# Half of the gate and z projections of one hybrid decoder layer computed by Strassen's scheme in 2 x 2 block pairs

## The reference, cut to what matters

```
hn    = rms_norm(x, norm_mix)                       # 1024 tokens x 1024 channels
proj  = hn @ w_in + b_in                            # x_rnn, z_rnn, q/k/v, z_att, gates
gates = sigmoid(proj[..., OFF_GATES:])              # 2 branches x 1024 channels
...
att   = sum over 3 groups of softmax(lse) * out     # merge of three dilated window patterns
y_att = att * silu(z_att)                           # 512 channels
merged = gates[0] * (y_rnn @ w_o_rnn) + gates[1] * (y_att @ w_o_att)
x = x + merged @ w_out                              # then a second, gated embedding branch
```

## Time and profile before

| | |
|---|---|
| median of 3 runs | 1344.41 us (1344.07 to 1344.48) |
| the profiled execution's own time | 1344.83 us |
| its span | 1343.0 us |
| TensorE busy, of the span | 1331.1 us (99%) |
| VectorE, ScalarE, POOL busy | 785.6, 507.7, 532.5 us |
| gate sigmoids (L827) start | 757.6 to 983.2 us |

### The profile page before, as it was taken

The page is one execution under the profiler, slowest core; times in us unless marked ns, Lnnn a source line. Parts: engine busy times, 40 slices in busy tenths (PEclk is TensorE's granted clock), DMA queues, the critical chain, the costliest instruction groups (busy, mean ns, idle before and its releaser), DMA issues.

```text
span 1343.0 us, 17645 instructions
## 1 busy us (share of the span) xinstructions
PE 1331.1 (99%) x6262; PEld 1104.2 (82%) x6262; DVE 785.6 (58%) x1257; ACT 507.7 (38%) x1282; POOL 532.5 (40%) x500
## 2 busy tenths in 40 slices
PE   8999999999999999999999999999999999999998
PEld 6887888888888888888888888888888888888887
DVE  6799888842779666565665752158612566234323
ACT  7455646542434444344443688311200011223100
POOL 6975424404458334041340632343067317044020
PEclk9999999999999999999999999999999999999999
DMA  6232312322202032120310332376279635122111
GB/s 239 79 102 87 105 60 79 110 100 72 75 12 83 24 91 64 32 83 20 99 56 33 114 93 92 100 244 212 94 270 413 201 127 155 57 79 63 40 47 47
DMA packets 84471, 139.51 MB, mean 104 GB/s; under 512 B 10048, under 2 KB 41120, under 8 KB 84384
## 3 DMA queue, kind: packets, MB, share of 16 engines
q10 hardware_dynamic: 39936, 75.82, 15.9%
q1 hardware_dynamic: 44448, 62.56, 15.6%
HBM read 108.84 MB, written 29.51 MB: 103 GB/s over the span
## 4 chain that ended last, share of the span: by engine, by line
PE 90%; DVE 5%; issue 1%; ACT 1%; POOL 1%; DMA 0%; SPq 0%; POOLq 0%; DVEq 0%; ACTq 0%
PE bank L1268 28%; PE bank L1273 28%; PE bank L1272 28%; PE bank L1425 2%; PE bank L1405 2%; PE bank L1392 1%; PE bank L1414 1%; DVE xc L1002 1%; PE bank L1518 1%; POOL ring L542 0%; ACT L743 0%; DMA raw<-in_w_rnn_s 0%; DVE qkr L1110 0%; DVE qks L1111 0%; DVE ibuf L1029 0%
## 5 line engine op out<-in xcount | busy, mean ns | idle before, releaser
L542 POOL TENSOR_TENSOR ring<-raw,ring 128x512 fp32r<-128x512 f32 x221 | 311.7, 1410 | 725.9 <-PE bank L1273 642.5
L1268 PE MATMUL bank<-hn,ring 128*128 128x512 f32 x640 | 251.7, 393 | 1.5 <-DVE sgbuf L990 1.2
L1273 PE MATMUL bank<-hn,ring 128*128 128x512 f32 x640 | 249.4, 390 | 0.0
L1272 PE MATMUL bank<-hn,ring 128*128 128x512 f32 x640 | 249.2, 389 | 0.0
L1268 PE MATMUL bank<-ring,hn 128*128 128x512 f32 x576 | 232.6, 404 | 0.2 <-POOL ring L542 0.2
L1273 PE MATMUL bank<-ring,hn 128*128 128x512 f32 x576 | 225.8, 392 | 0.0
L1272 PE MATMUL bank<-ring,hn 128*128 128x512 f32 x576 | 225.2, 391 | 0.0
L546 POOL TENSOR_SCALAR ring<-raw 128x512 fp32r<-128x512 f32 x221 | 183.7, 831 | 8.4 <-DMA raw<-in_w_rnn_s 8.3
L1268 PEld LDWEIGHTS bank<-hn,ring 128*128 128x128 f32 x640 | 120.2, 188 | 26.7 <-DVE sgbuf L990 1.6
L1273 PEld LDWEIGHTS bank<-hn,ring 128*128 128x128 f32 x640 | 120.1, 188 | 25.3
L1272 PEld LDWEIGHTS bank<-hn,ring 128*128 128x128 f32 x640 | 120.2, 188 | 24.1
(11 more groups left out here) (182 smaller groups left out, 2151.9 us busy)
## 6 DMA issues: line engine op xcount, KB each, us to landing
raw<-in_w_tail_s SPq DMA_DIRECT2D x104, 256.0 KB, 2.7
g_in<-gate_dram ACTq DMA_DIRECT2D x48, 256.0 KB, 3.6
raw<-in_w_rnn_s SPq DMA_DIRECT2D x45, 256.0 KB, 2.6
raw<-in_w_qkv_s SPq DMA_DIRECT2D x48, 192.0 KB, 2.4
gate_dram<-g_out ACTq DMA_DIRECT2D x32, 256.0 KB, 2.1
raw<-in_w_qkv_s SPq DMA_DIRECT2D x48, 128.0 KB, 2.2
o_dram<-o_buf ACTq DMA_DIRECT2D x48, 128.0 KB, 1.8
o_in<-o_dram ACTq DMA_DIRECT2D x12, 512.0 KB, 3.9
```

What stands on the lines that cost most here:

```text
L542: nc.gpsimd.tensor_tensor(ring[:, ring_slot(p), 1], raw[:, p % RAW], ring[:, ring_slot(p), 0].bitcast(F32), ALU.subtract).then_inc(w_ready, 1)
L1268: ins = T.matmul(out, lhs[0], rhs[0], start=first, stop=False)
L1272: T.matmul(out, lhs[0], rhs[1], start=False, stop=False)
L1273: return T.matmul(out, lhs[1], rhs[0], start=False, stop=last)
```

## The change

The first eight gate tiles (`PLAIN`) stay as they are, in 16 slots. The other eight gate tiles and the four z tiles are taken two at a time, in six pairs (`PAIRS`): two output tiles by two token halves, with the 8 channel blocks split 4 and 4. Such a 2 x 2 by 2 x 2 product needs 8 block products; the change computes it with 7 (`PRODUCTS`), each of 4 blocks x 3 matmuls, from sums and differences of quadrants.

- Activation quadrants: VectorE makes three combinations per channel block (`combine`, 7 operations of 128 x 512 for each k, two after each of the attention steps that lie in gate slots), POOL cuts them into hi and lo in ring slots 4 to 15 (`combined_parts`, 6 operations each). A fourth combination overwrites a quadrant of `hn` (`combine_last`, 5 VectorE operations for each of 4 blocks).
- The ring has four slots for the gates and pairs (`RING_PAIR`).
- Weight quadrants: a pair's four pieces are loaded together (`load_pair`); POOL makes four sums in place in `raw`. From the fifth product on, ScalarE makes the hi part of each product's weights (`weight_hi`), POOL the lo part.
- Products go round eight banks. ScalarE copies the first product of a pair to `part_sum`; VectorE adds the others (7 additions per pair) into the four outputs, from which ScalarE takes the sigmoids.
- The merge steps are placed by a table (`MERGE_AT`) behind products 10 to 34, the merge weights at product 3. The weights are now stored by class, so that the multiplication in `merge_step` is one contiguous operation. The loads of `o_in`, `wt_in`, the statistics and merge weights move from ScalarE's queue to SP's, between the pairs' weight loads.

```diff
+PLAIN = 8
+GATE_ORDER = [(t, h) for t in range(PLAIN - 2) for h in range(2)] + [(t, h) for h in (1, 0) for t in (PLAIN - 2, PLAIN - 1)]
+PAIRS = [("z", 0), ("z", 2)] + [("gate", t) for t in range(PLAIN, 2 * KD, 2)]
+PRODUCTS = 7
+MERGE_AT = {10 + 9 * i // 4: i for i in range(UNITS)}
+ROWS_AT = 3
...
@@ sync @@
+            def load_pair(u):
+                for r in range(RAWS):
+                    sp.wait_ge(w_ready, FIRST_PAIR + PRODUCTS * (u - 1) + 3 + r + 1)
+                    load(raw_of(u, r), a["w_tail_s"][FIRST_PAIR - FIRST_TAIL + RAWS * u + r])
...
+            load_pair(1)
+            sp.wait_ge(mw_done, 1)
...
+            load_parts(0, 2)
+            load_pair(2)
+            load_parts(2, 4)
+            load_pair(3)
+            load_parts(4, 7)
+            load_pair(4)
+            load_parts(7, 10)
+            load_pair(5)
+            load_parts(10, UNITS)
@@ gpsimd @@
+                for r in range(2):
+                    pool.wait_ge(raw_in[slots[r]], pair_count(u, r))
+                    cut(r, r)
+                for r in (2, 3):
+                    pool.wait_ge(raw_in[slots[r]], pair_count(u, r))
+                G.tensor_tensor(a21, a21, a22, ALU.add).then_inc(pair_sum, 1)
...
+                G.tensor_tensor(a11, a21, a11, ALU.subtract).then_inc(pair_sum, 1)
...
+                G.tensor_tensor(a12, a12, a11, ALU.subtract).then_inc(pair_sum, 1)
...
+                cut(2, 0)
+                G.tensor_tensor(a11, a22, a11, ALU.subtract).then_inc(pair_sum, 1)
+                cut(3, 1)
+                cut(4, 0)
+                cut(5, 2)
+                cut(6, 3)
@@ scalar @@
+            for m in range(PRODUCTS * len(PAIRS) + 2):
+                u, i = divmod(m, PRODUCTS)
+                if u < len(PAIRS):
+                    act.wait_ge(prod_done, m + 1)
+                    if i == 0:
+                        if u >= 1:
+                            act.wait_ge(*pair_taken(u - 1, 0))
+                        nc.scalar.activation(part_sum[:, 0], pair_bank(u, 0)[:], ACT.Copy).then_inc(prod_kept, 1)
+                    if m + RING_PAIR < PRODUCTS * len(PAIRS):
+                        weight_hi(m + RING_PAIR)
...
+                    if i == 4:
+                        take_pair(u, 0)
+                if u >= 1 and i == 0:
+                    take_pair(u - 1, 1)
+                    take_pair(u - 1, 2)
+                if u >= 1 and i == 1:
+                    take_pair(u - 1, 3)
@@ vector @@
+                if i == 2:
+                    dve.wait_ge(prod_kept, u + 1)
+                    if u >= 1:
+                        dve.wait_ge(*pair_taken(u - 1, 2))
+                    link(V.tensor_tensor(u_sum, pair_bank(u, 2)[:], first, ALU.add))
+                    V.tensor_tensor(first, pair_bank(u, 1)[:], first, ALU.add).then_inc(prod_sum, 1)
...
+                if m in MERGE_AT:
+                    merge_step(MERGE_AT[m])
+                    if MERGE_AT[m] % GROUPS == GROUPS - 1:
+                        finish_head(MERGE_AT[m] // GROUPS)
@@ tensor @@
+            for m in range(PRODUCTS * len(PAIRS)):
+                u, i = divmod(m, PRODUCTS)
...
+                    pe.wait_ge(*product_taken(m - 8))
...
+                c = FIRST_PAIR + m
+                need(c)
+                moving = pair_moving(i)
+                for k in range(KD // 2):
+                    ins = passes(pair_bank(u, i)[:], part(c, slice(k * P, (k + 1) * P)), moving(k),
+                                 k == 0, k == KD // 2 - 1)
+                ins.then_inc(prod_done, 1)
+                used[0] = 1
```

More of the change, by code:

```diff
@@ L107, with combined_ops @@
 MAIN_ORDER = main_order()
-Q_STAT = 15
+Q_STAT = 14
+Q_FREE = GATE_ORDER.index((PLAIN - 1, 1))
+def combined_ops(A):
+    first = SLOTS_Q * KD
+    free = [a for a in range(STEPS) if FIRST_STEP + STEP_BLOCKS * a >= first]
+    if A not in free:
+        return range(0)
+    i = free.index(A)
+    return range(min(2 * i, 7 * KD // 2), min(2 * i + 2, 7 * KD // 2))
+COMBINE_AFTER = (5, 7, 9, 13)
+MERGE_AT = {10 + 9 * i // 4: i for i in range(UNITS)}
+ROWS_AT = 3
 P_CUT = (2, 4)
@@ L452, in evacuated @@
             if n < N_O:
-                q = n - N_Z
-                kind = Z_MAIN[q][0]
-                done = sum(1 for m in Z_MAIN[:q + 1] if m[0] == kind)
-                return (gate_done if kind == "gate" else za_done), done
+                return gate_done, n - N_Z + 1
             if n < N_W:
@@ L1116, in _ @@
                     attention(G)
+                    for j in combined_ops(G):
+                        combine(j)
                     continue
```

437 lines of the change are left out of this document (304 added, 133 removed).

## The result

| | kernel before | changed kernel |
|---|---|---|
| time, median of the comparison | 1344.41 us | 1368.3 us |
| lowest to highest run | 1344.07 to 1344.48 | 1368.23 to 1372.28 |
| profiled execution: time, span | 1344.83, 1343.0 | 1368.27, 1366.4 |

The ratio is 1.0183 with a 95% interval of 1.0171 to 1.0196: 24 us slower, where 1330.0 us and 14 us faster were forecast. The case that came true is the second rival, and it was worse than its 1356 us.

A forecast was written before the change was run, and what follows sets the result against it. TensorE's number of matmuls times their pace was taken as the bound. 1344.83 - 16.3 saved + 2 for waits gave 1330.5 us profiled; the median, 0.42 us lower, was forecast at 1330.0 us, range 1327.5 to 1340.

The forecast's parts named there:

- the second rival: Also rival 2: in the merge stretch VectorE and POOL shut each other out, 28 us surplus, 1356 us; chance 0.09.
- The saving: Six pairs on TensorE drop 72 matmuls at 0.2267 us, saving 16.3 us; a pair takes 19.04 us.
- the weighing of the rule: VectorE's two-SBUF-input instructions block POOL's SBUF reads, or the reverse; judged contradicted at 904.44, where both seemed to run at once.
- Its sign, a mean of POOL above 2 us: POOL's mean operation time in the pairs: above 2 us would show mutual exclusion; 1.4 to 1.6 was expected for lo parts.
- POOL's margin of 1.75 us: POOL's 11 operations per pair: TensorE waits only above about 1.75 us an operation; the mean was taken as 1.565.
- VectorE's drift "under the 8 us": Merge stretch: VectorE has 73 us of work in 68, drifts some 5 us behind, and may be 8 us late.
- ScalarE's waits for its sums: In the pairs ScalarE waits for VectorE's sums with the next hi part queued behind; cost 0.
- The combinations at cost 0: Beside the last attention steps, VectorE's two operations, 1.5 us, fit its 2.81 us idle per step; cost 0.
- SP's queue: Third pair's weights, issued at 29 to 31 us behind merge loads, cost 1 us of the 2 us charged.
- "Later pairs have their merge loads early enough": Pairs after the third: their merge loads come early enough in SP's queue, so no late weights were charged.
- The hand-over at 0 to 0.5 us: Output stage's start: gate loads go 3.3 us later, leaving 0.3 of 3.8 us; cost 0, at worst 0.5.

The follow-up runs named there:

- e4: Changed kernel with POOL's sums and lo parts in the pairs on 8 columns instead of 512; 1348.97 us, ratio 1.0025.
- e2: Changed kernel without the combinations of input blocks beside the attention steps, products reading plain blocks instead; 1364.47 us, ratio 1.015.
- e3: Changed kernel with most of VectorE's merge left out and all loads kept; 1350.21 us, ratio 1.0047.
- e9: Changed kernel with POOL's earlier order up to the first gate, no input-block combinations, and POOL's pair operations on 8 columns; 1338.97 us, ratio 0.996.
- e5: Changed kernel with POOL's sums and lo parts of the pairs replaced by zero fills that read nothing; 1348.19 us, ratio 1.0025.
- e6: Changed kernel with the merge's multiplies and adds on VectorE reading one tile instead of two; 1354.94 us, ratio 1.007.

## Why the prediction was wrong, point by point

**The saving was right.** 72 matmuls are gone, and at 0.2267 us they are worth 16.3 us. Where nothing is waited for, a pair does take the 19.04 us of the forecast: the first four pairs of e4 do. In the changed kernel they take 20.2, 22.8, 26.1 and 20.7 us.

**The step that failed is the weighing of the rule.** I took "at 904.44 both ran at once" from the earlier trace rows: two z multiplications in 3.20 us, and POOL's lo part of 1.53 inside them. But what do they take alone? In e4 the multiplication's mean is 1098 ns, so two take 2.20 us. 2.20 and POOL's 1.29 are 3.49, and the row shows 3.20. The row was a turn-taking with 0.29 us at its seams, within what the 70 pairs above show, and not an overlap; the wait was inside the duration, since an engine that is shut out counts as busy. The same holds for the means that I used as prices: 1229 for 1098, 1468 for 1225, 2486 for 2222. They already held a little exclusion, at a POOL load of 30%, and I carried them over to one of 80%. So the overlap of the two engines is the step that failed: they were added to the stage as if side by side, and the runs showed them taking turns, 82.6 and 51.8 us of lone work in 138 us.

Rival 2 had the right mechanism with 28 us of surplus in 68 us, and the pair stage lost 27.1 us. That the two numbers are so near is partly luck: 4.3 of the 27.1 us are the lower clock, and rival 2's 11.3 us a head is 12.4 at the prices of the earlier trace rows and leaves out the z sums. Its time of 1356 us was 12 us short; the losses outside the stage, which it didn't have, are 12.6 us. Its sign, a mean of POOL above 2 us, did not show either: the mean was 1.75. Its chance of 0.09 hung on one misread row.

**POOL's margin of 1.75 us was about right, and was reached.** The mean of its 64 operations was 1.75 us, but it was 1.88 and 1.94 in the two sets of six ahead of the long waits, and TensorE waited ten times, 16.4 us. With the merge thinned POOL's lo parts have a mean of 1.39, and the stage takes 127.8 us. Neither engine alone is the bound.

**VectorE's drift "under the 8 us" was wrong** in the same way: 73 us of work in 68 was worked out at the durations of a quiet neighbour. It stayed full to the end and was the body of the chain of waits. The path that I had named and costed at nothing, ScalarE's waits for its sums, held TensorE once, for 2.3 us. What I had not seen is that the merge loads in SP's queue, behind which the weights stand, wait for VectorE in turn.

**The combinations at cost 0 were wrong by 6.3 to 6.6 us.** The 2.81 us idle of a step did hold the two operations. What I left out is the stretching of the attention's own norm and rotation beside POOL's 4 x 6 added operations: from 770 to 840 us the norm's instructions have a mean of 683 ns, and 400 in e2.

**POOL's order up to the first gate** wasn't in the sum at all, though the diff shows it: 2.8 to 2.9 us in the span, 3.1 to 3.5 in the time.

**SP's queue was charged at 2 us for late weights.** They came later than forecast: the merge weights were ready 27.6 us after product 0 and not near 21, and the third pair's first weight load was issued after 33.6 us and not 29 to 31. In e4, where POOL alone was changed, the same two are 19.9 and 25.9 us, so this too comes from VectorE beside POOL: the merge weights' subtractions (L1372, 32 x 128) have a mean of 1407 ns, and 340 in e4. "Later pairs have their merge loads early enough" was wrong for the fifth pair. Neither e3 nor e4 moved those loads, and both brought the stage to within 3 to 8 us of what was to be had. What late weights alone cost was not tested by itself.

**The hand-over at 0 to 0.5 us was wrong**: TensorE waited 3.5 us for the last sums here, 2.0 in e4 and 2.3 in e9, and in e9 another 3.5 for the first gated sum. The lower clock after most of these waits came on top; after e4's it stayed at 1.00.

## What to carry to other kernels

Before work is added to VectorE or POOL, add up for the stretch the lone durations of VectorE's instructions with two SBUF inputs and of POOL's that read SBUF. If the sum comes near the length of the stretch, these two engines are one engine there, however idle each looks by itself. An operand from a bank, a reduction with a single input, or a fill did not count here; a cast with a single input did (last paragraph). And an engine's duration is no proof of overlap: compare it with the same instruction where the neighbour rests, before reading two rows side by side as parallel work.

## What the runs showed of the hardware that was not expected

A wait of TensorE costs more than itself. In the changed kernel the idle times of 4.3, 4.2 and 3.5 us in and behind the pairs each led to a stretch at half the clock, that is 1.2 GHz (all engines, columns as in the first windows above):

```profile
916.00:918.00 2.00, 2.00 (x7) 1.57 (x6) 1.97 (x2) 0.00 (x0) 2.00 (x1) 0.54 0.00 0
962.00:966.00 4.00, 3.77 (x9) 3.03 (x10) 3.93 (x6) 1.78 (x2) 4.00 (x4) 0.50 0.49 157
1006.00:1008.00 2.00, 2.00 (x6) 1.57 (x5) 0.00 (x0) 1.48 (x2) 1.85 (x3) 0.50 0.21 45
```

By the granted clocks of the windows of 2 us around them the three stretches cost some 6 us together, and they lie inside the losses above. The length of the wait alone does not tell: at the hand-over TensorE idled 2.0 us in e4 and in e5, and went on at 1.00 in e4 but at 0.59 and 0.56 in the next two windows in e5. The executions of e4 spread from 1342.61 to 1351.02 us, where those of the kernel before, in the same comparison, lie within 1.1 us. Such stretches can make only a part of that: two executions of e4 with a mean granted clock of 0.999 took 1348.78 and 1349.16 us. The rest of the spread stays open, since only one execution of each kernel was traced.

VectorE's cast of 1024 columns with one SBUF input takes 694 ns alone (e4), little more than half of the 1225 ns of the two-input instruction behind it. In the changed kernel its mean is 1186: two of the four take 693 and 696 ns, and two, beside POOL's operations, 1676 and 1680. So one SBUF input did not keep this instruction clear of POOL, unlike the reduction of e6 at 1212 ns. The Trainium skill, "SBUF — State Buffer", "Who interferes with whom", says that copies and casts can enter modes that use both ports, and then contend; the two blocked casts agree, though no row here names an instruction's mode.
